# Layer 1 of a two-layer hybrid block: the second and third branch work on the latent columns only, where the context's are not read

## The reference, cut to what matters

```python
def mlstm_mixer(zx, zc, b_i, b_f, g_norm, with_ctx):          # second branch
    ...
        h_c, state_ctx = mlstm_chunkwise(*in_c, state0)        # the context's state is read
        h_x, _ = mlstm_chunkwise(*in_x, state_ctx)
    ...
    out_x = mlstm_out(hs_x[0] + hs_x[1], cols_x[3], g_norm)    # cols[3]: output gates
    if not with_ctx:
        return out_x, None

def rwkv7_scan(r, decay, k, v, kk, a, s0):                     # third branch
    def step(s, inp):
        r_t, w_t, k_t, v_t, kk_t, a_t = inp
        sa = jnp.einsum('bhij,bhj->bhi', s, -kk_t)
        s = (s * w_t[..., None, :] + sa[..., :, None] * (kk_t * a_t)[..., None, :]
             + v_t[..., :, None] * k_t[..., None, :])
        return s, jnp.einsum('bhij,bhj->bhi', s, r_t)          # r is read for the output alone

def rwkv_out(y, bonus, gl, g2, lnx_w, lnx_b):
    ...                                                        # normalise y over each head
    g = jax.nn.sigmoid(gl) @ g2
    return (yn + bonus).reshape(B, T, H * N) * g
```

## Time and profile before

| what | us |
|---|---|
| median of 3 runs | 2910.65 (2905.84 to 2913.16) |
| the profiled execution's own time | 2912.04 |
| its span, first to last instruction | 2910.1 |
| PE busy | 2590.5 (89%) |
| DVE busy | 845.4 (29%) |
| ACT busy | 598.0 (21%) |
| layer 1's second and third branch | about 1766 to 2126 of the span |

### The profile page before, as it was taken

One profiled execution on the slowest core, in us unless ns is written; L12 is line 12 of the kernel. 1 busy time (PEld: TensorE's weight loads), 2 busy tenths in 40 slices (PEclk: granted clock), 3 DMA queues, 4 the chain that ended last, 5 costly groups with the idle time before them and its releaser, 6 DMA issues.

```text
span 2910.1 us, 38778 instructions
## 1 busy us (share of the span) xinstructions
PE 2590.5 (89%) x15936; PEld 1429.8 (49%) x15936; DVE 845.4 (29%) x1977; ACT 598.0 (21%) x1176; POOL 170.2 (6%) x178
## 2 busy tenths in 40 slices
PE   6999988999997999899898499989999798887874
PEld 2466467744446444344343356657878633332333
DVE  1254455311116231111112533454421521111114
ACT  3344132110002111111111243333120211111111
POOL 0000000000000111111111000000000011111110
PEclk8999988999996899999999699989999799898997
DMA  7111032421104499999996620112232499999993
GB/s 291 38 43 37 29 117 89 168 94 60 55 0 188 164 371 423 392 416 402 376 407 239 278 80 19 48 41 107 90 149 84 190 377 418 425 419 417 411 397 137
DMA packets 74559, 617.38 MB, mean 212 GB/s; under 512 B 17678, under 2 KB 17678, under 8 KB 32016
## 3 DMA queue, kind: packets, MB, share of 16 engines
q1 hardware_dynamic: 50192, 564.52, 47.7%
q0 software_dynamic: 24192, 50.39, 4.6%
HBM read 604.87 MB, written 47.71 MB: 224 GB/s over the span
## 4 chain that ended last, share of the span: by engine, by line
PE 84%; DVE 6%; issue 4%; DMA 4%; ACT 2%; SPq 0%; POOLq 0%; DVEq 0%; ACTq 0%; POOL 0%
PE bank L1757 21%; PE bank L1772 10%; PE bank L1243 9%; PE bank L286 7%; PE bank L1258 3%; PE bank L1248 3%; PE bank L1747 3%; PE bank L364 2%; DMA arena<-expert_rows 2%; PE bank L976 1%; PE bank L961 1%; PE bank L434 1%; PE bank L416 1%; PE bank L258 1%; PE bank L303 1%
## 5 line engine op out<-in xcount | busy, mean ns | idle before, releaser
L1757 PE MATMUL bank<-ring,arena 128*64 128x512 f32 (+1 forms) x1648 | 588.2, 631 | 101.1 <-issue 95.3
L1757 PEld LDWEIGHTS bank<-ring,arena 128*64 128x64 f32 (+1 forms) x1648 | 203.5, 158 | 424.3 <-issue 423.2
L1243 PE MATMUL bank<-normed,ring 128*128 128x512 f32 (+1 forms) x768 | 255.5, 486 | 0.0
L1757 PE MATMUL bank<-branches,arena 128*64 128x512 f32 (+1 forms) x528 | 251.5, 632 | 0.0
L1935 DVE TENSOR_TENSOR arena<-bank,arena 128x256 f32<-128x256 f32 x83 | 35.2, 424 | 705.8 <-ACT arena L1859 705.8
L1681 POOL DMA_INDIRECT arena<-hidden_rows,block_slots x81 | 82.3, 1016 | 2292.3 <-DVE block_slots L1510 1685.5
L1243 PEld LDWEIGHTS bank<-normed,ring 128*128 128x128 f32 x768 | 145.9, 190 | 102.2 <-issue 92.3
L286 PE MATMUL bank<-normed,ring 128*128 128x512 f32 x448 | 194.4, 593 | 0.0
L1859 ACT ACTIVATE arena<-bank 128x256 f32<-128x256 f32 x83 | 31.9, 384 | 688.3 <-PE bank L1757 688.3
L1772 PE MATMUL bank<-ring,arena 128*64 128x512 f32 (+1 forms) x560 | 163.4, 597 | 1.3 <-DVE arena L1941 1.3
L1772 PE MATMUL bank<-arena 128*64 128x512 f32 (+1 forms) x528 | 139.9, 604 | 1.1 <-ACT arena L1862 1.1
(11 more groups left out here) (430 smaller groups left out, 3581.8 us busy)
## 6 DMA issues: line engine op xcount, KB each, us to landing
ring<-in_wexp SPq DMA_DIRECT2D x96, 2048.0 KB, 19.4
ring<-in_wst SPq DMA_DIRECT2D x54, 2048.0 KB, 7.7
branches<-in_wexp SPq DMA_DIRECT2D x34, 2048.0 KB, 22.4
ring<-in_wexp SPq DMA_DIRECT2D x66, 1024.0 KB, 22.3
arena<-in_wexp SPq DMA_DIRECT2D x64, 1024.0 KB, 21.7
arena<-expert_rows SPq DMA_DIRECT2D x12, 2048.0 KB, 7.3
ring<-in_wst SPq DMA_DIRECT2D x4, 1536.0 KB, 11.5
hidden_rows<-arena SPq DMA_DIRECT2D x6, 512.0 KB, 2.6
```

Source lines behind the costliest of these rows:

```text
L1243: last = nc.tensor.matmul(ps[2 * (n % 4)][:, c0:], wg[:, k, i * P:(i + 1) * P], H[:, k, c0:], start=(k == 0), stop=(k == KD - 1))
L1757: last = nc.tensor.matmul(ps[2 + s][r0:r1, :], XT_[:, s, k * P + r0:k * P + r1], wt[:, k, :], start=(k == 0), stop=(k == KD - 1))
```

## The change

In layer 1 the work below is cut to the latent columns (256 of 512), or left out for the four context chunks. Layer 0 keeps its shapes.

- second branch: projections of queries and of both output-gate tiles; the stabiliser matmuls and their copies; the gates' copies and sigmoids
- third branch: projections of tiles 0, 1 and 8 with their copies and token mixing; the r half of `AR`; the r columns of the context chunks' scores and their masks; the y matmuls of the four context chunks in each direction; everything behind the scan

```diff
-        def project(pe, bank, weights, j0, n):
+        def project(pe, bank, weights, j0, n, c0=0):
-                last = nc.tensor.matmul(bank, weights[:, k, j0:j0 + n], H[:, k, :], start=(k == 0), stop=(k == KD - 1))
+                last = nc.tensor.matmul(bank[:, c0:], weights[:, k, j0:j0 + n], H[:, k, c0:], start=(k == 0), stop=(k == KD - 1))
...
-                project(pe, ps[j][:, :], front, j * P, P).then_inc(ml["z"], 1)
+                project(pe, ps[j][:, :], front, j * P, P, (1 - j) * queries_from(l)).then_inc(ml["z"], 1)
...
-            project(pe, ps[4][:, :], tail, 0, P).then_inc(ml["z"], 1)
+            project(pe, ps[4][:, :], tail, 0, P, queries_from(l)).then_inc(ml["z"], 1)
...
-                nc.tensor.matmul(ps[MB_BANK[u % 2]][:, :], cn("sel", P, u * P), RT[:, 1, :], start=True, stop=True).then_inc(ml["mb"], 1)
+                nc.tensor.matmul(ps[MB_BANK[u % 2]][:, t0 * P:], cn("sel", P, u * P), RT[:, 1, t0 * P:], start=True, stop=True).then_inc(ml["mb"], 1)
...
-                nc.scalar.activation(MbS[:, u % 2, :], ps[MB_BANK[u % 2]][:, :], ACT.Copy).then_inc(ml["mbs"], 1)
+                nc.scalar.activation(MbS[:, u % 2, c0:], ps[MB_BANK[u % 2]][:, c0:], ACT.Copy).then_inc(ml["mbs"], 1)
...
+        def first_half(l, j):
+            return 1 if l and j in (0, 1, 8) else 0
+        def score_cols(l, c):
+            return C if l and c < NC // 2 else 2 * C
...
-                project(pe, ps[j % 4][:, :], cols(n, KD), (j % 4) * P, P).then_inc(rw["z"], 1)
+                project(pe, ps[j % 4][:, :], cols(n, KD), (j % 4) * P, P, first_half(l, j) * TC).then_inc(rw["z"], 1)
...
-                                last = nc.tensor.matmul(ps[SC_BANK[pr][g]][h, (c % 4) * P:(c % 4 + 1) * P], src[h, c * C:(c + 1) * C],
-                                                        AR[pr][h, c, :], start=True, stop=True)
+                                n = score_cols(l, c)
+                                last = nc.tensor.matmul(ps[SC_BANK[pr][g]][h, (c % 4) * P:(c % 4) * P + n], src[h, c * C:(c + 1) * C],
+                                                        AR[pr][h, c, 0:n], start=True, stop=True)
...
                     for pr in PAIRS:
+                        if c * C < queries_from(l):
+                            continue
                         S0 = ST[pr][:, i % 2, :]
...
-                nc.tensor.matmul(ps[pr][:, :], bd, KDS[:, pr, :], start=True, stop=True).then_inc(rw["bs"], 1)
+                nc.tensor.matmul(ps[pr][:, c0:], bd, KDS[:, pr, c0:], start=True, stop=True).then_inc(rw["bs"], 1)
...
-                    ch.add(nc.vector.tensor_tensor(AR[pr][:, :, 64:128], by_chunk(Zs[:, pr, :]), by_chunk(ex3[pr]), ALU.mult))
+                    ch.add(nc.vector.tensor_tensor(AR[pr][:, n0:, 64:128], by_chunk(Zs[:, pr, c0:]), by_chunk(ex3[pr][:, c0:]), ALU.mult))
...
-                        nc.vector.tensor_copy(YA[:, pr, :], ps[pr][:, :]).then_inc(rw["yc"], 1)
+                        nc.vector.tensor_copy(YA[:, pr, c0:], ps[pr][:, c0:]).then_inc(rw["yc"], 1)
```

More of the change, by code:

```diff
@@ L675, in ml_act @@
         def ml_act(act, ch, l):
+            c0 = queries_from(l)
             act.wait_ge(ml["ab"], l * ML["ab"] + 1)
@@ L683, in ml_act @@
                 q = slice(32 * h, 32 * h + 32)
-                nc.scalar.activation(zq[h][q, :], ps[0][q, :], ACT.Copy, scale=float(MLQK) ** -0.5).then_inc(ml["zev"], 1)
+                nc.scalar.activation(zq[h][q, c0:], ps[0][q, c0:], ACT.Copy, scale=float(MLQK) ** -0.5).then_inc(ml["zev"], 1)
             act.wait_ge(ml["z"], l * ML["z"] + 3)
@@ L690, in ml_act @@
             act.wait_ge(ml["z"], l * ML["z"] + 6)
-            nc.scalar.activation(so[:, 0, :], ps[4][:, :], ACT.Copy).then_inc(ml["oev"], 1)
+            nc.scalar.activation(so[:, 0, c0:], ps[4][:, c0:], ACT.Copy).then_inc(ml["oev"], 1)
             act.wait_ge(ml["ra"], l * ML["ra"] + 2)
@@ L694, in ml_act @@
             act.wait_ge(ml["z"], l * ML["z"] + 7)
-            nc.scalar.activation(so[:, 1, :], ps[5][:, :], ACT.Copy).then_inc(ml["oev"], 1)
+            nc.scalar.activation(so[:, 1, c0:], ps[5][:, c0:], ACT.Copy).then_inc(ml["oev"], 1)
             def stabiliser(u):
@@ L725, in ml_act @@
                 act.wait_ge(ml["oev"], l * ML["oev"] + i + 1)
-                nc.scalar.activation(so[:, i, :], so[:, i, :], ACT.Sigmoid).then_inc(ml["so"], 1)
+                nc.scalar.activation(so[:, i, c0:], so[:, i, c0:], ACT.Sigmoid).then_inc(ml["so"], 1)
             for i, ts in enumerate(halves(l)):
@@ L1021, in rw_pe @@
             pe.wait_ge(rw["bo"], l * RW["bo"] + 1)
+            c0 = queries_from(l)
             for pr in range(2):
-                nc.tensor.matmul(ps[pr][:, :], bd, KDS[:, pr, :], start=True, stop=True).then_inc(rw["bs"], 1)
+                nc.tensor.matmul(ps[pr][:, c0:], bd, KDS[:, pr, c0:], start=True, stop=True).then_inc(rw["bs"], 1)
             for pr in range(2):
-                last = nc.tensor.matmul(ps[2 + pr][:, :], bd, YA[:, pr, :], start=True, stop=True)
+                last = nc.tensor.matmul(ps[2 + pr][:, c0:], bd, YA[:, pr, c0:], start=True, stop=True)
                 last.then_inc(rw["ym"], 1)
             for pr in range(2):
-                nc.tensor.matmul(ps[6 + pr][:, :], WS[:, WS_G2 + pr * P:WS_G2 + (pr + 1) * P], Zs[:, 8, :], start=True, stop=True).then_inc(rw["g"], 1)
+                nc.tensor.matmul(ps[6 + pr][:, c0:], WS[:, WS_G2 + pr * P:WS_G2 + (pr + 1) * P], Zs[:, 8, c0:], start=True, stop=True).then_inc(rw["g"], 1)
             for pr in range(2):
                 pe.wait_ge(rw["yq"], l * RW["yq"] + pr + 1)
-                nc.tensor.matmul(ps[4 + pr][:, :], bd, sq_[pr], start=True, stop=True).then_inc(rw["ys"], 1)
+                nc.tensor.matmul(ps[4 + pr][:, c0:], bd, sq_[pr][:, c0:], start=True, stop=True).then_inc(rw["ys"], 1)
         sq_ = (beta[0], kappa[0])
@@ L1041, in rw_act @@
                     act.wait_ge(rw["pad"], l * RW["pad"] + 1)
-                dst = ZP[:, j % 2, :].rearrange("p (s t) -> p s t", s=2)[:, :, 1:257]
-                nc.scalar.activation(dst, ps[j % 4][:, :].rearrange("p (s t) -> p s t", s=2), ACT.Copy).then_inc(rw["zev"], 1)
+                half = first_half(l, j)
+                dst = ZP[:, j % 2, :].rearrange("p (s t) -> p s t", s=2)[:, half:, 1:257]
+                nc.scalar.activation(dst, seg(ps[j % 4][:, :])[:, half:, :], ACT.Copy).then_inc(rw["zev"], 1)
             act.wait_ge(rw["sh"], l * RW["sh"] + 9)
             nc.scalar.activation(Zs[:, 6, :], Zs[:, 6, :], ACT.Tanh).then_inc(rw["tl"], 1)
-            nc.scalar.activation(Zs[:, 8, :], Zs[:, 8, :], ACT.Sigmoid).then_inc(rw["tl"], 1)
+            c0 = queries_from(l)
+            nc.scalar.activation(Zs[:, 8, c0:], Zs[:, 8, c0:], ACT.Sigmoid).then_inc(rw["tl"], 1)
             act.wait_ge(rw["kc"], l * RW["kc"] + 1)
@@ L1101, in rw_dve @@
             for j in range(9):
-                z = ZP[:, j % 2, :].rearrange("p (s t) -> p s t", s=2)
+                half = first_half(l, j)
+                z = ZP[:, j % 2, :].rearrange("p (s t) -> p s t", s=2)[:, half:, :]
                 dve.wait_ge(rw["zev"], l * RW["zev"] + j + 1)
-                t = seg(tsh)
+                t = seg(tsh)[:, half:, :]
                 if j:
@@ L1108, in rw_dve @@
                 ch.link(nc.vector.tensor_scalar(t, t, hmu[:, j:j + 1], None, ALU.mult))
-                nc.vector.scalar_tensor_tensor(seg(Zs[:, j, :]), z[:, :, 1:257], omu[:, j:j + 1], t, ALU.mult, ALU.add).then_inc(rw["sh"], 1)
+                nc.vector.scalar_tensor_tensor(seg(Zs[:, j, :])[:, half:, :], z[:, :, 1:257], omu[:, j:j + 1], t, ALU.mult, ALU.add).then_inc(rw["sh"], 1)
             dve.wait_ge(rw["sh"], l * RW["sh"] + 9)
@@ L1157, in rw_dve @@
                         dve.wait_ge(rw["sc"], l * RW["sc"] + 8 * d + 4 * pr + g + 1)
-                        dst = (MB if g < 2 else MK)[pr][:, 4 * (g % 2):4 * (g % 2) + 4, :]
-                        nc.vector.tensor_tensor(dst, ps[SC_BANK[pr][g]][:, :].rearrange("p (c t) -> p c t", c=4),
-                                                bcast(mask, 1, 4), ALU.mult).then_inc(rw["msk"], 1)
+                        n = score_cols(l, 4 * (g % 2))
+                        dst = (MB if g < 2 else MK)[pr][:, 4 * (g % 2):4 * (g % 2) + 4, 0:n]
+                        nc.vector.tensor_tensor(dst, ps[SC_BANK[pr][g]][:, :].rearrange("p (c t) -> p c t", c=4)[:, :, 0:n],
+                                                bcast(mask[:, 0:n], 1, 4), ALU.mult).then_inc(rw["msk"], 1)
                 for pr in PAIRS:
```

24 lines of the change are left out of this document (13 added, 11 removed).

## The result

| what | before, us | changed, us |
|---|---|---|
| median of 4 runs each | 2909.05 (2905.84 to 2913.16) | 2861.97 (2856.45 to 2865.28) |
| the profiled execution's own time | 2912.04 | 2862.72 |
| its span | 2910.1 | 2860.6 |

The ratio is 0.9836, 95% interval 0.9815 to 0.9856: the changed kernel is faster by 47.1 us, where 37.0 were forecast.

The account below looks back on a forecast made before the run. The prediction took PE to bound the kernel, with 84% of the span hanging on it. Its terms summed to 37.0 us off the profiled 2912.04, making 2875.0; it forecast 2874 us, range 2863 to 2886.

Parts of the forecast that it names:

- Terms 1 to 4: Second branch's projections 10.3 us, its stabilisers 3.4, third branch's projections 10.3, gap behind tile 8 1.2, all saved.
- terms 1 and 2: Second branch: three projected tiles at half the columns save 10.3 us, eight stabiliser matmuls at half save 3.4 us.
- term 3: Third branch: projections of tiles 0, 1 and 8 on half the columns save 10.3 us.
- Terms 5 and 6: Third branch: halving the r half of `AR` saves 0.6 us, the narrower score matmuls 3.3 us.
- Term 7: Scans: leaving out y saves 0.25 us in each of 8 context steps, 2.0 us; lower bound 0.
- Term 8: Behind the scans: L1197, L1199 and L1203 save 1.45 us, the last four pairs of matmuls 4.4 us.
- The covers: Waits said to stay hidden: L672's by 0.8 us, the merge's for the third branch's result (L1220) by 1.7 us.
- rival C: A cover breaks (L672, L1220) or the second branch's units are bound by the engines' round: 2881 us, chance 0.06.
- The clock: PE's half clock for 14.6 us behind tile 8: a possible 7.3 us gain not counted; no fall expected in scans.
- Rival B: Gap behind tile 8 ends before the clock falls, or slow stretch at least halves: 4 to 7.3 us more, chance 0.11.
- Rival A: The clock falls inside the emptier scans: typical price 9 us, 2883 us, chance 0.13.
- sign of being wrong: The forecast is wrong if the stretch from 1766 to 2126 shrinks by less than 30 or more than 45 us.

Follow-up runs that it names:

- ml_only: The kernel before with only the second branch's cuts (projections, stabilisers, copies, sigmoids): 2888.47 us, ratio 0.9946.
- proj_only: The kernel before with only the third branch's tiles 0, 1 and 8 projected, copied, mixed and passed through the sigmoid on latent columns: 2892.03 us, ratio 0.9952.
- y_only: The kernel before with only the y matmuls of the four context chunks in each direction left out: 2896.68 us, ratio 0.9983.
- tail_only: The kernel before with only what follows the scans in layer 1 cut to the latent columns: 2897.88 us, ratio 0.9982.
- before_fill: The kernel before with matmuls that nothing reads added in four empty PE gaps of layer 1's third branch: 2895.23 us, ratio 0.9961.
- before_y_late: The kernel before with each scan step's y matmuls moved one step later, in both layers: 2896.29 us in one run.

## What the forecast had right, and which step failed

- **Terms 1 to 4, projections, stabilisers and the gap**, 25.2 us: they measure 25.2 (10.2, 3.6, 10.2 and 1.1, rounded), and terms 1 and 2 come out alone in `ml_only`, term 3 and the gap in `proj_only`. The price per column read from L605 holds, and all of it was on the path.
- **Terms 5 and 6, AR and scores**, 3.9 us: a pair's 64 score records take 2.71 us (32 of each width) instead of 3.52 in the chain, 3.2 us for the four pairs of both directions. No experiment had them alone, and in their stages they can't be told from the clock.
- **Term 7, the scan's y**, 2.0 us: mis-sized. It measures 3.3 us, 0.41 a step instead of 0.25, the same in `y_only` and in the changed kernel. From the state's copy to the next `rh` it gave 0.31 us (1.16 to 0.85), a little more than the 0.25 that I took from a place with an empty queue. The other 0.10 stands ahead in the step: from the copy of `uu` to the state's copy it is 0.89 us where a step with another's y ahead has 1.00, so PE comes to the state's matmuls earlier too. The upper bound of 0.7 a step, y's own PE time, held.
- **Term 8**: 1.5 us were forecast and measured for the copies. The four pairs gave 4.6 us for 4.4: the forecast is half of a length that held 3.4 us at 0.50, and the changed kernel's 3.90 us hold none. With the slow stretch left in, `tail_only` has 5.37.
- **The covers** (rival C) held: L672 without a wait, the units at 3.51 us each where they were 3.94 (1810.69 to 1814.20 in the chain), no wait of PE in the merge for the third branch's result, and the merge and the rest the same within 0.2 us of the means.
- **The clock** was the step that failed. The prediction put it at nothing ("I do not count on it") and left every slow stretch as long as before. In the four stages that carry them the means fell by 8.0 us where terms 5 and 6 had 3.9. These stages hold 43 and 36 us at 0.50 in the two traces of before, and 17, 31, 28 and 20 in the four of the changed kernel. Of the 4 us that no term had, 1.5 are shown to be the clock's: they fell behind tile 8, where all four traces agree, and `before_fill` shows that the clock is worth 3.25 us there. The other 2.5 us fell in direction 1, where I had looked at no clock at all. There the clock is the likeliest cause (13.5 us before and 10.5 in the two traces with 0.2 and 0.3 us at 0.50), but about 0.4 us go with the rarer pauses, and with a scatter of 3 us and two traces against four the amount isn't shown.
- **Rival B** had the place behind tile 8 right and its reason and price wrong. The clock still fell in the gap or right at its end. The slow time went from 17.4 to 8.6 us, the half that B asks for, and gave 1.5 us, not 4 to 7.3. I had read the earlier trace rows as if PE bound all of it (14.58 busy of 14.60). With the clock up, the chain goes over to ACT and DVE, PE is busy for 11.04 of 18.85 us, and 5.3 us of the slow time that is left fall on an empty PE.
- **Rival A** (clock falling in the scans) didn't come: no record of a scan is at 0.50 in any of the traces, with 2.39 us steps as with 2.82. PE's gaps within a scan are at most 0.54 us long. The Trainium skill, TensorE: Matmul & The Clock Gate, section "HAM oscillation — how this bites in real kernels", describes a loop that is throttled again and again at waits of about 3 to 5 us and so doesn't speak of gaps this short. The gap behind tile 8, 5.17 to 6.28 us long, agrees with it: the clock fell in it, or within 0.1 us of its end, in each of the twelve traces that leave it unfilled.
- **The base.** 47.1 us were measured where the stages' means have 42.7. The other 4.4 are a difference between executions: the first trace of before has 1.5 us more in the branches than the mean of its two, the first of the changed kernel 2.9 less than the mean of its four.

So 37.0 of some 43 us stand in the terms: 1.3 more are the scan's, about 3.5 the clock's (1.5 of them shown), about 0.4 the pauses', the rest is rounding. The 12 us between the forecast's 2874 and the measured 2861.97 are 1.6 us of base (2910.65 against 2909.05), these 6, and 4 that did not come back in later runs. Those 4 are chance, and without them the median would lie inside the range. The prediction's own sign of being wrong, more than 45 us in the two branches, is met by the first pair of traces (47.1) and not by the means (42.7).

Open: what decides whether a slow stretch begins, and when it ends. The shorter gap goes with the shorter slow time in each of the six traces that have it unfilled, but `y_only` and `before_y_late` have it shorter with the long gap (8.8 and 13.4 us at 0.50). An edit that moves PE's work in time seems to shift where the clock falls; that is argued, not shown.
